# Three resident query tiles, a ring of ten rows and single-row value sums in a two-layer attention and expert-mixer step

## The reference

```python
def trunk_layer(x, cond, rope, ctx, lp, lambda_init, alpha):
    mod = jax.nn.silu(cond) @ lp['w_mod'] + lp['b_mod']
    sh1, sc1, g1, sh2, sc2, g2 = jnp.split(mod[:, None, :], 6, axis=-1)
    h = layer_norm(x) * (1.0 + sc1) + sh1
    mix, own_ctx = mixers(h, rope, ctx, lp, lambda_init)   # three attention groups, one in- and one out-projection
    x = layer_norm(alpha * x + g1 * mix, lp['ln1_g'], lp['ln1_b'])
    h = layer_norm(x) * (1.0 + sc2) + sh2
    ff = peer_ffn(h, lp['peer_wq'], lp['peer_keys'], lp['peer_u'], lp['peer_v'])
    x = layer_norm(alpha * x + g2 * ff, lp['ln2_g'], lp['ln2_b'])
    return x, own_ctx
```

```python
        u = jnp.take(u_tab, eb, axis=0)
        act = jax.nn.gelu(jnp.einsum('td,tkd->tk', xb, u))
        return jnp.einsum('tk,tkd->td', gb * act, jnp.take(v_tab, eb, axis=0))
```

## Time and profile before

| what | value |
|---|---|
| median of three runs | 2481.61 us |
| profiled execution, span (the profile gives no other time of this execution) | 2660.3 us |
| mean granted TensorE clock | 0.790 |
| PE busy | 1716.3 us (65%) |
| DVE busy | 1616.4 us (61%) |
| POOL busy | 1491.3 us (56%) |
| ACT busy | 337.3 us (13%) |
| moved by DMA | 980.68 MB, of it 847.35 MB by the queue of POOL (gathers and modulation tiles), 130.80 MB by that of SP |

### The profile page before, as it was taken

The page is one execution under the profiler, slowest core; times in us unless marked ns, Lnnn a source line. Parts: engine busy times, 40 slices in busy tenths (PEclk is TensorE's granted clock), DMA queues, the critical chain, the costliest instruction groups (busy, mean ns, idle before and its releaser), DMA issues.

```text
span 2660.3 us, 24559 instructions
## 1 busy us (share of the span) xinstructions
PE 1716.3 (65%) x8433; PEld 893.7 (34%) x8433; DVE 1616.4 (61%) x3949; ACT 337.3 (13%) x998; POOL 1491.3 (56%) x1583
## 2 busy tenths in 40 slices
PE   6886759676376666366577585867638667435556
PEld 4564514342143422222344342435214342000101
DVE  3266775676865673954467964547866566854441
ACT  1320013101120100002110101311112010000000
POOL 1105466655656465566455664555665666766664
PEclk8987877888578778687688797788757878777779
DMA  8969899999999999999899999889999999999997
GB/s 315 422 252 364 314 389 367 390 370 394 368 328 401 358 411 413 404 411 410 314 366 387 369 411 355 317 336 354 410 380 328 395 379 411 389 357 377 364 367 296
DMA packets 248333, 980.68 MB, mean 369 GB/s; under 512 B 28001, under 2 KB 29681, under 8 KB 232849
## 3 DMA queue, kind: packets, MB, share of 16 engines
q0 software_dynamic: 226944, 847.35, 82.1%
q1 hardware_dynamic: 19536, 130.80, 12.3%
q10 hardware_dynamic: 1728, 0.95, 0.1%
HBM read 976.47 MB, written 2.52 MB: 368 GB/s over the span
## 4 chain that ended last, share of the span: by engine, by line
PE 17%; issue 12%; POOL 9%; DMA 8%; another core or an unknown queue 8%; DVE 7%; ACT 1%; SPq 0%; DVEq 0%; ACTq 0%; POOLq 0%
POOL expert L660 9%; PE acc L968 6%; DMA expert<-in_experts,eidx_t 4%; DVE expert L1529 3%; PE mmb L911 2%; DMA expert<-in_experts,eidx 2%; PE mmb L779 2%; PE mmb L860 1%; PE ob L887 1%; DMA wt<-in_w_wq 1%; PE trb L867 1%; PE mmb L743 1%; ACT hT L1048 1%; DVE small L1216 0%
## 5 line engine op out<-in xcount | busy, mean ns | idle before, releaser
L660 POOL DMA_INDIRECT expert<-in_experts,eidx x768 | 736.1, 958 | 648.0 <-PE acc L968 261.2
L1529 DVE CUSTOM_DVE_ANT_0 expert<-expert,hb 128x1024 f32<-128x1024 f32 x768 | 904.3, 1218 | 268.1 <-DMA expert<-in_experts,eidx 211.2
L660 POOL DMA_INDIRECT expert<-in_experts,eidx_t x768 | 730.5, 951 | 329.7 <-issue 212.5
L968 PE MATMUL acc<-expert,strip 128*32 128x512 f32 x3072 | 710.8, 725 | 262.2 <-DMA expert<-in_experts,eidx_t 190.5
L968 PEld LDWEIGHTS acc<-expert,strip 128*32 128x32 f32 x3072 | 135.0, 123 | 737.5 <-DMA expert<-in_experts,eidx_t 399.5
L911 PE MATMUL mmb<-hT,wt 128*128 128x128 f32 x1472 | 211.8, 307 | 58.2 <-issue 31.4
L911 PEld LDWEIGHTS mmb<-hT,wt 128*128 128x128 f32 x1472 | 200.3, 220 | 86.7 <-issue 68.9
L769 PE MATMUL mmb<-wt,hT 128*128 128x244 f32 x736 | 178.6, 404 | 33.4 <-issue 12.9
L769 PEld LDWEIGHTS mmb<-wt,hT 128*128 128x128 f32 x736 | 152.8, 211 | 64.6 <-issue 35.3
L1399 DVE TENSOR_REDUCE neg_max<-mmb 128x1 f32<-128x384 f32 (+1 forms) x120 | 55.1, 466 | 165.1 <-PE mmb L860 83.5
L942 PE MATMUL trb<-ident,acts 128*128 128x128 f32 x24 | 9.6, 398 | 171.0 <-DVE acts L1549 100.9
(11 more groups left out here) (192 smaller groups left out, 1629.8 us busy)
## 6 DMA issues: line engine op xcount, KB each, us to landing
wt<-in_w_wq SPq DMA_DIRECT2D x46, 1152.0 KB
expert<-in_w_mod POOLq DMA_DIRECT2D x39, 1024.0 KB, 13.8
wt<-in_w_win SPq DMA_DIRECT2D x30, 976.0 KB
wt<-in_w_wout SPq DMA_DIRECT2D x24, 1024.0 KB
expert<-in_experts,eidx POOLq DMA_INDIRECT x768
expert<-in_experts,eidx_t POOLq DMA_INDIRECT x768
wt<-in_w_mod SPq DMA_DIRECT2D x8, 1024.0 KB
wt<-in_w_uq SPq DMA_DIRECT2D x6, 384.0 KB
```

Source lines behind the costliest of these rows:

```text
L660: pool.indirect_dma_start(expert[:, g % RING, :], None, table, bass.IndirectOffsetOnAxis(at, 0)).then_inc(landed[g % RING], 16)
L968: m = pe.matmul(acc[32 * i:32 * i + 32, cs], strip[:, q % 2, i, at:at + 32], expert[:, (g + i) % RING, cs], start=k < 4, stop=False, skip_ ...
L1529: v.tensor_tensor_reduce(expert[:, r, :], expert[:, r, :], hb[:], 1.0, 0.0, ALU.mult, ALU.add, dots[:, k:k + 1]).then_inc(dot_ready, 1)
```

## The change

`RING` goes from 15 to 10. Three tiles of `wq` (`HELD`, numbers 1, 4 and 6) get a place in SBUF, `held`, and are loaded once a layer, for the prompt, and read again by blocks 1 and 2. `rows` moves into `area` and has 3 rows; ACT waits for `rows_used` before it writes the next block's `q_t` over it. `gain` holds one layer and is loaded again for layer 1. The start uses 5 pairs of ring slots, `wide` and two `held` places first, then the 5 pairs alone.

v rows are taken one at a time, one v and one u by turns (`BLEND`), and `column()` goes. Each row now belongs to one quarter of the columns' width per column group: four matmuls of 256 columns, one in each column group, all of the same row. `acc` so holds the sum in another layout, and a new step `out` on ACT copies it to `tmp` in 8 pieces of 32 x 256 per half: the first half after 116 v rows, the second before `fin`. `fin` 0 reads `tmp`.

```diff
-RING = 15
+RING = 10
-RROWS = 2
+RROWS = 3
+HELD = (1, 4, 6)
-BLEND = "u" * LEAD + ("vvvv" + "uuuu") * ((SLOTS - LEAD) // 4) + "v" * (SLOTS - (SLOTS - LEAD))
+BLEND = "u" * LEAD + "vu" * (SLOTS - LEAD) + "v" * LEAD
+GROUP = 32 // TOKS
+OUT_AT = 3 * PART + 2 * GROUP + 4
...
+    if kind == "wq" and i in HELD:
+        return WRING + 3 + HELD.index(i)
...
+        if kind == "route" and e in HELD and b > 0:
+            next(y for y in tiles if y[0] == ("wq", l, e))[2] = i + 1
+        elif kind == "route" and e < WQ_T:
             tiles.append([("wq", l, e), i, i + 1])
...
-        rows = sb("rows", [P, RROWS, D])
+        held = sb("held", [P, len(HELD), WT])
-        gain = sb("gain", [P, L, G_N])
+        gain = sb("gain", [P, G_N])
+        rows = cut(area, KV, (RROWS, D))
...
-            if k <= MOD_RING:
+            if k < FIRST:
                 return k, 1
...
+                        sp.dma_start(gain[:], t_in["gain"][n].partition_broadcast(P)).then_inc(gain_in, 16)
...
-                        at = eidx_t[:, part(l, b), column(k):column(k) + 1]
+                        at = eidx_t[:, part(l, b), k:k + 1]
...
-                    for k in range(k0, k0 + cnt, 4):
+                    for k in range(k0, k0 + cnt):
                         g = slot + k - k0
-                        q, c = k // PART, k % PART // 4
+                        q, j = divmod(k, PART)
+                        blk, at = j // GROUP, 32 * (j % GROUP)
...
-                        at = 32 * c
-                        for half, i in itertools.product(range(2), range(4)):
-                            cs = slice(half * 512, half * 512 + 512)
-                            if half == 0:
-                                pe.wait_ge(landed[(g + i) % RING], 16 * ((g + i) // RING + 1))
-                            m = pe.matmul(acc[32 * i:32 * i + 32, cs], strip[:, q % 2, i, at:at + 32],
-                                          expert[:, (g + i) % RING, cs], start=k < 4, stop=False,
+                        pe.wait_ge(landed[g % RING], 16 * (g // RING + 1))
+                        for c in range(4):
+                            m = pe.matmul(acc[32 * c:32 * c + 32, 256 * blk:256 * blk + 256], strip[:, q % 2, blk, at:at + 32],
+                                          expert[:, g % RING, 256 * c:256 * c + 256], start=first, stop=False,
                                           skip_group_check=True)
-                            if half == 1:
-                                m.then_inc(slot_done, 1)
+                        m.then_inc(slot_done, 1)
...
+                    act.wait_ge(rows_used, n("rows", 0))
...
+                if kind == "out":
+                    act.wait_ge(slot_done, SLOTS * (3 * l + b) + (3 * PART + 2 * GROUP if e == 0 else SLOTS))
+                    for blk, c in itertools.product((2 * e, 2 * e + 1), range(4)):
+                        m = act.activation(tmp[32 * blk:32 * blk + 32, 256 * c:256 * c + 256],
+                                           acc[32 * c:32 * c + 32, 256 * blk:256 * blk + 256], ACT.Copy)
+                    m.then_inc(acc_read, 1)
...
-                        v.wait_ge(slot_done, SLOTS * (3 * l + b + 1))
-                        v.tensor_tensor(z, acc[:], r, ALU.mult).then_inc(acc_read, 1)
-                        v.wait_ge(acc_read, n("acc"))
+                        v.wait_ge(acc_read, 2 * (3 * l + b) + 2)
+                        link(v.tensor_tensor(z, z, r, ALU.mult))
```

More of the change, by code:

```diff
@@ L77 @@
         "qm_t": 1, "cache_t": 2, "kv_mla": 5, "heads": 2, "mix": 1, "wout": 3.6, "ln_x": (2.5, 5.2, 2.5),
-        "ln_h": 5.2, "route": 1.5, "topk": 4.7, "pick": (4.4, 6.5, 4.4, 6.5), "fin": (1.3, 6.5, 2.5), "idx_t": 1}
+        "ln_h": 5.2, "route": 1.5, "topk": 4.7, "pick": (4.4, 6.5, 4.4, 6.5), "fin": (1.3, 6.5, 2.5), "idx_t": 1, "out": 1.5}
 def cost_of(x):
@@ L209, in gathers_to @@
                 out.append(("act", l, "", b, acts_due.pop() // PART - 1))
+            if kind == "v" and count[kind] == OUT_AT:
+                out.append(("out", l, "", b, 0))
             if kind == "u" and count[kind] % PART == 0:
@@ L223, in fins @@
 def fins(l, b):
-    return [("fin", l, "", b, i) for i in range(3)]
+    return [("out", l, "", b, 1)] + [("fin", l, "", b, i) for i in range(3)]
 def early_mod(x):
@@ L499, in trunk_program @@
         tile_slots = [wt[:, i, :] for i in range(WRING)] + [area[:, KV + i * WIN:KV + (i + 1) * WIN] for i in range(2)]
-        tile_slots += [area[:, 0:WT]]
+        tile_slots += [area[:, 0:WT]] + [held[:, i, :] for i in range(len(HELD))]
         first_norm = {1: wide[:, WIN:WIN + D], 2: wide[:, WIN + D:WIN + 2 * D]}
         def mod_place(k):
-            if k <= MOD_RING:
+            if k < FIRST:
                 return k, 1
-            return (k - 1 - MOD_RING) % MOD_RING, (k - 1 - MOD_RING) // MOD_RING + 2
+            return (k - FIRST) % MOD_RING, (k - FIRST) // MOD_RING + 2
         def mod_slot(k):
@@ L512, in mod_slot @@
                 return wide[:, 2048:4096]
+            if i > MOD_RING:
+                return held[:, i - MOD_RING - 1, 0:2048]
             return expert[:, 2 * i:2 * i + 2, :].rearrange("p a d -> p (a d)")
         const_in = sem("const_in")
+        gain_in = sem("gain_in")
         cache_in = sem("cache_in")
-        w_in_slot = [sem(f"w_in_slot{i}") for i in range(WRING + 3)]
+        w_in_slot = [sem(f"w_in_slot{i}") for i in range(len(tile_slots))]
         cond_in = sem("cond_in")
@@ L524, in trunk_program @@
         mod_added = sem("mod_added")
-        mod_landed = [sem(f"mod_landed{i}") for i in range(MOD_RING + 1)]
+        mod_landed = [sem(f"mod_landed{i}") for i in range(FIRST)]
         first_ready = sem("first_ready")
@@ L685, in weights @@
                 tile += 1
+                if at_held is not None:
+                    held_in[at_held] = tile_slots[at_slot]
                 return tile_slots[at_slot]
```

53 lines of the change are left out of this document (30 added, 23 removed).

## The result

The changed kernel takes 2534.65 us (2527.83 to 2545.07 in four runs) against 2481.47 of the kernel before: 1.0206 times as long, interval 1.0182 to 1.023. (A ratio with its interval is estimated from all executions of both kernels; it can differ by 0.2% from the quotient of the two medians.) The forecast was 2464, faster; the time lies in the stated range of 2420 to 2540, near that of rival A (2529).

What follows compares the result with a forecast made beforehand. The prediction took transfers as the bound, the kernel running at nine tenths of what they allow. Terms −31 − 8 − 22 + 30 + 10 + 2 = −19 gave 2641.3 us profiled, times 0.9328 = 2464 us; range 2420 to 2540.

Steps and rivals of the forecast that it cites:

- rival A: Ring of ten runs dry after long waits: 43 on DVE, 25 on PE; total +51, 2529 us, slower; chance 0.30.
- the ring term: Ten slots for fifteen: less cover while DVE or PE is away from its rows; +30, bounds 0 and +105.
- single rows: v rows freed one by one spread POOL's waits for PE: −22 of 54 us lost around ten waits, bounds 0 and −44.
- The 6.5 us on the way: Time from the last row's issue on POOL to its use by PE, taken as time its slot is useless.
- Matmuls of 256 columns: PE's v rows: a group of four costs 0.22 to 0.24 us more; +10, bounds 0 and +60.
- The end: Chain after the last issue: eight copies +3.1, last row's matmuls about −1.2; +2, bounds −1 and +4.
- Fewer bytes: Query tile loads, 36 for 48, 14.16 MB less: −31, bounds −34.6 and −12.
- The −8 for waits: PE's 12.5 us of waits for query tiles shrink by two thirds: −8, bounds −16 and 0.
- Rival B: No change: saved bytes lie in routing where DMA waits for PE, only −12 real; 2481.6 us; chance 0.20.
- The signs it gave: For the ring: more POOL idle time on DVE's dots, and u-stretch windows (1060 to 1080) below a share of 1.03.
- Two signs of being wrong: Waits on `acc` don't fall in sum; the DMA's mean rate falls by more than the 1.4% of bytes.
- Rival C: A larger gain: the ring costs nothing, a row needing under 5.2 of ten slots; −49, 2436 us; chance 0.08.

Runs made afterwards that it cites:

- second profile: The kernel before, run once more with no edit, to get another profile of it: 2493.33 us, profiled span 2491.5 us.

## Why the prediction was wrong, point by point

**The steps that failed: the ring term, and single rows.** The sum had −31 − 8 − 22 + 30 + 10 + 2. Measured against it:

| step | in the sum (profiled time) | measured | from |
|---|---|---|---|
| fewer bytes and waits for tiles | −39 | −30 | held tiles at ring 10 |
| ten slots for fifteen | +30 | +64 (single rows), +62 (groups) | ring 15 against 10 |
| single rows, 256 columns, the end | −10 | +17 | single rows at ring 15 |

*Ten slots for fifteen*: that fewer slots give less cover was right; the size was half of what it is, and the place was wrong. The sum let u rows lose 6.2 us of cover and v rows only 1.2. The 6.5 us on the way drop out of that difference; what made it small is the 4 x 1.245 = 5.0 us of a group, taken off the cover of v rows before and not after. So single rows were credited with most of what five slots are worth, and the ten waits for v rows cost 6 us in the sum. The runs show no such credit: the ring costs 64 us with single rows and 62 in groups, and two thirds of the lost transfer stand beside waits for PE.

The 6.5 us itself was too short, though that leaves the sum as it is: it was read where POOL had paused shortly before. At the end of a kernel, with nobody away, the distance from the last row's issue to its use by PE grows with the ring. The lines are the last gather and PE's weight load for it, with ten slots (the changed kernel), twelve, fifteen (single rows) and fifteen (the kernel before, second profile):

```profile
2508.06 0.93 POOL L670 DMA_INDIRECT expert<-in_experts,eidx_t  x1 [0.30 <-issue]
...
2518.86 0.20 PEld L984 LDWEIGHTS acc<-expert,strip 128*32 128x32 f32 x8 [1.03 <-DMA expert<-in_experts,eidx_t]
```

```profile
2492.46 0.93 POOL L670 DMA_INDIRECT expert<-in_experts,eidx_t  x1 [0.30 <-issue]
...
2505.71 0.16 PEld L984 LDWEIGHTS acc<-expert,strip 128*32 128x32 f32 x8 [1.09 <-DMA expert<-in_experts,eidx_t]
```

```profile
2460.43 0.94 POOL L670 DMA_INDIRECT expert<-in_experts,eidx_t  x1 [0.30 <-issue]
...
2477.82 0.20 PEld L984 LDWEIGHTS acc<-expert,strip 128*32 128x32 f32 x8 [1.04 <-DMA expert<-in_experts,eidx_t]
```

```profile
2463.71 0.94 POOL L660 DMA_INDIRECT expert<-in_experts,eidx_t  x1 [0.46 <-PE acc L968]
...
2477.45 0.16 PEld L968 LDWEIGHTS acc<-expert,strip 128*32 128x32 f32 x8 [1.10 <-DMA expert<-in_experts,eidx_t]
```

The distances are 10.8, 13.3, 17.4 and 13.7 us. With single rows each slot more adds 1.3 us, the transfer of one row: the rows of the ring wait in line for their transfer. That line is what the DMA lives on while PE or DVE is away. Five rows less are 5 x 1.28 = 6.4 us less of it. The runs show what this comes to: 16 to 21 dips of 3 to 5 us each, and the curve, 22 us a slot from 10 to 12 and 7 from 12 to 15. Why the curve bends is an argument only: a deep ring leaves few absences that empty it.

*Single rows* had a gain of 22 us from fewer lumps, out of 54 us of lost transfer around ten waits. Those 54 us were read in a profiled execution that was 7% longer than the runs. In the second profile the part after 420 us runs at 408 GB/s and loses 3.5 us, so next to nothing is left to smooth. The waits did become shorter, as the order on PE let expect: in the changed kernel the longest wait of POOL for PE's v rows is 9.3 us where it was 17.9 and, undisturbed, 11.9. Between the two orders the gain is real as well, 24 us in the form with 256 columns, but only against a loss which that form brings itself. The error is to have taken the losses of that one execution for the kernel's; scaling the sum by 0.9328 didn't mend it, since it shrinks every term a little and leaves the 54 us in.

*Matmuls of 256 columns* was +10, from 0.22 us more for a group. The trace shows none of it: six rows in 2.80 us are 0.47 a row at a granted clock of 1.00, against 0.48 in groups, and doubling these matmuls adds nothing to the time. What the form does change is the granted clock. The prediction didn't mention it.

*The end* was +2; it is +6.6. From the end of PE's last v row to `fin` 0 there are 7.56 us with single rows at ring 15, and 0.12 in the kernel before, first single rows, then before:

```profile
2477.82 1.08 PE L984 MATMUL acc<-expert,strip 128*32 128x256 f32 x8 [0.15 <-DMA expert<-in_experts,eidx_t]
...
2486.46 1.23 DVE L1589 TENSOR_TENSOR tmp<-tmp,area 128x1024 f32<-128x1024 f32 x1 [56.35 <-ACT tmp L1205]
```

```profile
2477.45 1.90 PE L968 MATMUL acc<-expert,strip 128*32 128x512 f32 x10 [0.20 <-DMA expert<-in_experts,eidx_t]
...
2479.47 1.22 DVE L1561 TENSOR_TENSOR tmp<-acc,rows 128x1024 f32<-128x1024 f32 x1 [49.95 <-PE acc L968]
```

Of these 7.4 us more, 3.1 are the copies, as forecast, and 4.3 the gate's row, whose slip the prediction had overlooked: the added step moved something that is placed by counting steps. The last row itself takes PE 0.8 us less. The rest of the 17 us lies in the gathers: from the first to PE's start on the last row there are 2264.4 us with single rows (213.40 to 2477.82) and 2255.4 before (222.08 to 2477.45), 9 more, as lost transfer rises by 9 (from 3.5 to 12). Which absence they come from isn't assigned.

*Fewer bytes* was right: −31 in the sum, 30 of 34.6 us measured. The −8 for waits doesn't show beside it. Rival B (hidden bytes, a third of them real) is excluded, since even where the ring is deep one tile gave 8 of its 11.5 us.

**What was right.** Rival A named the ring and had 0.30, and its 68 for the ring is close. That its 2529 is so near is luck in part: it put 43 of the 68 on DVE and 25 on PE, where two thirds stand beside waits for PE, and its +20 for PE's matmuls isn't there, while single rows cost about as much by the end and the gathers. The signs it gave came true: windows in the u stretches below 1.03, POOL's waits for the dots up from 106 (136 in the second profile) to 198 us. Two signs of being wrong came true only against the second profile: the sum of the waits on `acc` rises from 259 to 270 us (it was 307 in the first), and the mean rate falls from 394 to 381 GB/s, 3.3% and not 1.4. Rival A's break-even, 2.9 us at each of 17 places, is 49 us; the ring costs more. Rival C is excluded by the ring's 64 us. The rule of the Trainium skill that stood beside it ("DMA: Bandwidth & Descriptors", section "Anatomy of one DMA — SWDGE (gpsimd) path") gives one transfer a fixed 2.0 us and its bytes at their rate, an estimate of 3.2 us by that page. From issue to use the trace has 10.8 us at full load, with the line of rows ahead in it.

## What to carry to other kernels

Where the transfers are the bound, the depth of a ring is, in this kernel, not only what a row needs on its way but a reserve for the absences of its readers, and slots are worth most where the ring is short: here 22 us each from 10 to 12. SBUF that buys fewer bytes by giving up ring slots must be priced by that curve (three tiles −30, five slots +64); one tile in space that was free otherwise gave 8 us. And before waits are added up, the profiled execution is to be held against the runs: one that is 7% longer shows waits that the kernel doesn't have.

## What had not been expected of the hardware

The mean granted clock follows how the v rows are cut, with the same sums (the two levels read as 1.00 and 0.50 in windows): 0.842 in groups of four (512 columns); 0.721 in single rows of 256 columns, and 0.717 with these in the order of before; 0.82 when the same single rows are worked twice; 0.916 when a row takes PE 1.21 us. With single rows in the changed kernel, PE is idle about 0.2 us between rows at the end (2498 to 2519), and about 1.5 us where u and v come by turns (2266 to 2298). Other matmuls on PE get longer with the low clock (scores of 32x384 from 575 to 885 ns); at a ring of 15 the time of the kernel hardly moves with it (5 us from 0.72 to 0.82, with the doubled work in it).
